# Two transformer blocks on one core: x normalised and modulated beside the memory units, the memory keys later, two more steps in each attention head, and the last norm's row loaded later

## The reference

```
# first block
mod = silu(c) @ w_ada + b_ada                 # 2048 x 12288: six rows of 2048
shift_m, scale_m, gate_m, shift_f, scale_f, gate_f = split(mod, 6)
h = rmsnorm(x, g_norm_mix) * (1 + scale_m) + shift_m
dq, dk, dv, q_lat, kv_lat, k_pe = split(h @ w_in)
o_diff = 8 heads: (softmax(q1 k1) - lam * softmax(q2 k2)) @ v, then a norm
q = rmsnorm(q_lat) @ w_q_b;  kv = rmsnorm(kv_lat) @ w_kv_b
o_mla = 8 heads: softmax(q k) @ v
x = x + gate_m * (concat(o_diff, o_mla) @ w_out)
h = rmsnorm(x, g_norm_ffn) * (1 + scale_f) + shift_f
x = x + gate_f * (square(relu(h @ w_ff1)) @ w_ff2)      # 2048 -> 8192 -> 2048
x = rmsnorm(x, g_final)
# second block
proj = rms_norm(x) @ w_in_2       # q, k, v, z of three branches and three gates of 2048
ya = 12 heads, sliding window of 128, with sinks
yb = 12 heads, causal with forgetting
mk, mv = split(rms_norm(mem) @ w_mem_kv)                # 256 memory tokens
yc = 4 heads: softmax(norm(qc) norm(mk)) @ mv
y = sum over branches of sigmoid(gate) * ((y_branch * silu(z)) @ w_branch)
out = x + y @ w_out_2
```

## Time and profile before

| | before |
|---|---|
| median of three runs | 2192.8 us (2191.8 to 2196.15) |
| profiled execution, its span | 2190.42 us, 2188.6 us |
| mean granted clock of TensorE | 0.961 |
| busy: PE, DVE, ACT, POOL | 2000.1 (91%), 1313.3 (60%), 945.3 (43%), 157.9 us (7%) |
| moved by DMA | 448.82 MB, 205 GB/s in the mean |
| memory tiles 15 and 16 done at | 93.1 and 96.6 us |
| x times rx on ScalarE (L698), first two pieces of eight | 1.33 us, from 95.35 |
| waits of PE on heads, 262 to 411.6 us, beside the one in the rows | 0.15, 2.52 and 1.64 us for pt; 1.48 for probs |
| waits of PE on heads of branches a and b | 2.63 for pt; 1.42 and 0.44 for probs; 2.59 for the reciprocal; 2.71 and 1.57 for z |
| PE busy in 620 to 660 us (first tiles of w_ff1) | 18.89 and 18.41 of 20 us each |

### The profile page before, as it was taken

How to read it: one execution, slowest core, us unless ns; L and a number is a source line. 1 busy time by engine, 2 the same in 40 slices (tenths; PEclk the granted TensorE clock), 3 DMA queues, 4 the chain that set the end, 5 groups by cost and what they waited for, 6 DMA issues and landing times. The chain is left out here.

```text
span 2188.6 us, 24524 instructions
## 1 busy us (share of the span) xinstructions
PE 2000.1 (91%) x9240; PEld 1642.4 (75%) x9240; DVE 1313.3 (60%) x2057; ACT 945.3 (43%) x1440; POOL 157.9 (7%) x118
## 2 busy tenths in 40 slices
PE   6598897867789999999999999979999999999999
PEld 3276775546667888888888878878988877787877
DVE  3777876776796555555555555566555545545544
ACT  2453445343444344434434455445444444444433
POOL 0100000001000110110010021110100001101000
PEclk9798999878999999999999999989999999999999
DMA  9798775657797555555555555434534456656644
GB/s 356 284 327 307 244 250 199 235 189 278 290 340 255 192 192 184 192 193 186 188 193 187 187 193 179 149 100 126 164 108 149 126 169 198 192 182 187 194 170 170
DMA packets 128967, 448.82 MB, mean 205 GB/s; under 512 B 14288, under 2 KB 14544, under 8 KB 128336
## 3 DMA queue, kind: packets, MB, share of 16 engines
q1 hardware_dynamic: 124928, 433.74, 59.8%
q0 software_dynamic: 1568, 7.34, 0.9%
q10 hardware_dynamic: 2352, 6.17, 0.7%
HBM read 443.00 MB, written 4.19 MB: 204 GB/s over the span
## 5 line engine op out<-in xcount | busy, mean ns | idle before, releaser
L283 DVE TENSOR_TENSOR wlo<-raw,whi 128x1024 fp32r<-128x1024 f32 (+4 forms) x652 | 784.9, 1208 | 750.3 <-ACT whi L282 695.5
L282 ACT ACTIVATE whi<-raw 128x1024 fp32r<-128x1024 f32 (+4 forms) x652 | 658.3, 1012 | 836.6 <-PE g L397 707.0
L392 PE MATMUL g<-whi,lhsA_hi 128*128 128x512 f32 (+4 forms) x1840 | 715.8, 391 | 35.6 <-DVE lhsA_lo L788 28.0
L393 PE MATMUL g<-whi,lhsA_lo 128*128 128x512 f32 (+4 forms) x1840 | 698.0, 381 | 0.0
L397 PE MATMUL g<-wlo,lhsA_hi 128*128 128x512 f32 (+4 forms) x1840 | 470.0, 378 | 0.2 <-DVE wlo L283 0.2
L392 PEld LDWEIGHTS g<-whi,lhsA_hi 128*128 128x128 f32 x1840 | 357.3, 194 | 99.0 <-ACT tmp L780 21.8
L393 PEld LDWEIGHTS g<-whi,lhsA_lo 128*128 128x128 f32 x1840 | 357.6, 194 | 53.8 <-issue 1.4
L397 PEld LDWEIGHTS g<-wlo,lhsA_hi 128*128 128x128 f32 x1840 | 344.4, 193 | 56.2 <-DVE wlo L283 0.4
L537 DVE SCALAR_TENSOR_TENSOR raw<-raw,srow 128x1024 f32<-128x1024 f32 x181 | 217.5, 1224 | 17.8 <-DMA raw<-in_w_ada 17.5
L392 PE MATMUL g<-whi,lhsF_hi 128*128 128x512 f32 x512 | 200.6, 392 | 0.0
L393 PE MATMUL g<-whi,lhsF_lo 128*128 128x512 f32 x512 | 199.4, 389 | 0.0
(11 more groups left out here) (250 smaller groups left out, 1471.8 us busy)
## 6 DMA issues: line engine op xcount, KB each, us to landing
raw<-in_w_ff SPq DMA_DIRECT2D x256, 512.0 KB, 3.5
raw<-in_w_ada SPq DMA_DIRECT2D x181, 512.0 KB, 4.8
raw<-in_w_in SPq DMA_DIRECT2D x176, 512.0 KB, 4.2
raw<-in_w_out SPq DMA_DIRECT2D x64, 512.0 KB, 5.0
raw<-in_w_in SPq DMA_DIRECT2D x80, 384.0 KB, 3.1
raw<-in_w_branch_a SPq DMA_DIRECT2D x12, 512.0 KB, 3.5
raw<-in_w_branch_b SPq DMA_DIRECT2D x12, 512.0 KB, 4.3
raw_wide<-in_w_ada SPq DMA_DIRECT2D x11, 512.0 KB, 7.6
```

The lines of the kernel that those rows point to most:

```text
L282: t_hi = AC.put(lambda e: e.activation(hi, x, ACT.Copy), landed, free, us=0.2 + n * 0.00167)
L283: t_lo = DV.put(lambda e: e.tensor_tensor(lo, x, hi.bitcast(F32), ALU.subtract), landed, t_hi, free, us=0.15 + n * 0.00208)
L392: PE.put(lambda e, o=o, x=xh, w=h, f=first: e.matmul(o, x, w, start=f, stop=False), w, mark=False, us=us)
L393: PE.put(lambda e, o=o, x=xl, w=h: e.matmul(o, x, w, start=False, stop=False), mark=False, us=us)
```

## The change

Four edits, no new arithmetic.

1. row_norms(xs) and the eight `modulated` generators are appended before the first memory unit is run, so that they run beside the memory units; a `modulated` step now also waits until its piece of xs is scaled. angles() and lam() stand behind the second memory unit. The memory keys (mem_keys) are appended behind both units, with four `yield`s more, so that they come in w_in.
2. In diff_head and in softmax_pv a `yield` is put ahead of taking bank T and another ahead of taking bank O; the same two in causal_head. Each head's chain is two steps longer.
3. g_final is no longer loaded beside x, but behind the eight adds of w_out, when spread(1) has been appended.

```
-    for j in range(8):
-        bg.append(mem_turned(j))
-    bg.append(row_norms(ms, t_m, ssm, rm, "rm"))
...
-    par, tok = run(u_mem[0], width=3, adas_per_pair=2)
-    drain()
-    r = take(rows)
-    ks = evac2(par, tok, 512, r.ap, t_of["rm"], r.free, scale=(rm[:, 0:1], rm[:, 1:2]))
-    bg.append(mem_keys(r, ks))
-    bg.append(row_norms(xs, t_x, ssx, rx, "rx"))
-    angles()
-    lam()
-    par, tok = run(u_mem[1], adas_per_pair=2)
-    t_of["mv"] = evac2(par, tok, 512, mv, t_of["rm"], scale=(rm[:, 0:1], rm[:, 1:2]))
-    narrow()
-    while ("xs", 3) not in t_of:
-        pump()
...
     def modulated(j, src, src_tok, sec, ready=None):
...
-        while any(c not in ada_done for c in cs):
+        while any(c not in ada_done for c in cs) or (sec == 0 and ("xs", j // 2) not in t_of):
             yield
...
     for j in range(8):
+        bg.append(mem_turned(j))
+    bg.append(row_norms(ms, t_m, ssm, rm, "rm"))
+    bg.append(row_norms(xs, t_x, ssx, rx, "rx"))
+    for j in range(8):
         bg.append(modulated(j, [xs[:, t, (2 * j + i) * P:(2 * j + i + 1) * P] for i in range(2) for t in range(2)],
                             lambda j=j: t_of["xs", j // 2], 0))
...
+    def mem_keys(r, tok):
+        yield from heads_norm(r, 4, 128, tok)
+        for _ in range(4):
+            yield
...
+    par, tok = run(u_mem[0], width=3, adas_per_pair=2)
+    while "rm" not in t_of:
+        pump(1, 3)
+    r = take(rows)
+    ks = evac2(par, tok, 512, r.ap, t_of["rm"], r.free, scale=(rm[:, 0:1], rm[:, 1:2]))
+    par, tok = run(u_mem[1], width=3, adas_per_pair=2)
+    t_of["mv"] = evac2(par, tok, 512, mv, t_of["rm"], scale=(rm[:, 0:1], rm[:, 1:2]))
+    narrow()
+    angles()
+    lam()
+    while ("xs", 3) not in t_of:
+        pump(1, 3)
+    bg.append(mem_keys(r, ks))
...
@@ reload
         x_tok.extend([t_xr] for _ in range(4))
-        t_of["gfin"] = load(PO, gfin, a["g_final"].rearrange("(a d) -> a d", a=1).to_broadcast([P, D]), w)
...
     bg.append(spread(1, [DV.tok()]))
+    t_of["gfin"] = load(PO, gfin, a["g_final"].rearrange("(a d) -> a d", a=1).to_broadcast([P, D]), fence)
```

More of the change, by code:

```diff
@@ L708, in mem_turned, with modulated @@
                    [t_vec])
+    def modulated(j, src, src_tok, sec, ready=None):
+        cs = [4 * sec + (sec // 2) * 4 + j // 2, 4 * sec + (sec // 2) * 4 + 4 + j // 2]
+        wanted[j] = cs
+        while any(c not in ada_done for c in cs) or (sec == 0 and ("xs", j // 2) not in t_of):
+            yield
+        b = yield from grab(SOB)
+        tok = turn_rows(b, src, src_tok())
+        yield
+        tm = yield from grab(tmps)
+        for i in range(2):
+            kk = 2 * j + i
+            gcol, scol = mods[:, 16 * (sec + 1) + kk:][:, 0:1], mods[:, 16 * sec + kk:][:, 0:1]
+            tt = AC.put(lambda e, i=i, g=gcol, s=scol: e.activation(
+                tm.ap[:, 256 * i:256 * i + 256], b.ap[:, 256 * i:256 * i + 256], ACT.Identity, bias=s, scale=g),
+                tok, tm.free, [ada_done[c] for c in cs])
+        b.release([tt])
+        hi = lhsA.hi[:, 2 * j:2 * j + 2, :].rearrange("p a b -> p (a b)")
+        lo = lhsA.lo[:, 2 * j:2 * j + 2, :].rearrange("p a b -> p (a b)")
+        th = AC.put(lambda e: e.activation(hi, tm.ap[:, :], ACT.Copy), tt, lhsA.free)
+        yield
+        tl = DV.put(lambda e: e.tensor_tensor(lo, tm.ap[:, :], hi.bitcast(F32), ALU.subtract), th, lhsA.free)
+        tm.release([tl])
+        lhsA.ready[j] = tl
     for j in range(8):
@@ L712, in build @@
     bg.append(row_norms(ms, t_m, ssm, rm, "rm"))
+    bg.append(row_norms(xs, t_x, ssx, rx, "rx"))
+    for j in range(8):
+        bg.append(modulated(j, [xs[:, t, (2 * j + i) * P:(2 * j + i + 1) * P] for i in range(2) for t in range(2)],
+                            lambda j=j: t_of["xs", j // 2], 0))
     def heads_norm(r, segs, width, tok, off=0):
@@ L752, in build @@
     par, tok = run(u_mem[0], width=3, adas_per_pair=2)
-    drain()
+    while "rm" not in t_of:
+        pump(1, 3)
     r = take(rows)
     ks = evac2(par, tok, 512, r.ap, t_of["rm"], r.free, scale=(rm[:, 0:1], rm[:, 1:2]))
-    bg.append(mem_keys(r, ks))
-    bg.append(row_norms(xs, t_x, ssx, rx, "rx"))
+    par, tok = run(u_mem[1], width=3, adas_per_pair=2)
+    t_of["mv"] = evac2(par, tok, 512, mv, t_of["rm"], scale=(rm[:, 0:1], rm[:, 1:2]))
+    narrow()
     angles()
     lam()
-    par, tok = run(u_mem[1], adas_per_pair=2)
-    t_of["mv"] = evac2(par, tok, 512, mv, t_of["rm"], scale=(rm[:, 0:1], rm[:, 1:2]))
-    narrow()
     while ("xs", 3) not in t_of:
-        pump()
-    def modulated(j, src, src_tok, sec, ready=None):
-        cs = [4 * sec + (sec // 2) * 4 + j // 2, 4 * sec + (sec // 2) * 4 + 4 + j // 2]
-        wanted[j] = cs
-        while any(c not in ada_done for c in cs):
[L772 to L790, removed]
-    for j in range(8):
-        bg.append(modulated(j, [xs[:, t, (2 * j + i) * P:(2 * j + i + 1) * P] for i in range(2) for t in range(2)],
-                            lambda j=j: t_of["xs", j // 2], 0))
+        pump(1, 3)
+    bg.append(mem_keys(r, ks))
     fence = [PE.tok(), AC.tok(), DV.tok(), PO.tok()]
```

## The result

The changed kernel takes 2214.4 us (median of four runs, 2209.8 to 2215.66), the kernel before 2192.3 (four runs). The ratio is 1.0094 with an interval of 1.0078 to 1.0110: 21 us slower, where 2184 was forecast, and outside the stated range.

The account below looks back on a forecast made before the run. TensorE, busy 2000 of 2188.6 us, was taken to bound the kernel. -3.6 - 8 + 10 - 2 - 4 - 1.5 = -9.1 us from 2190.4 gives 2181.3; the median lies 2.4 higher, so 2184, range 2170 to 2202.

Parts of the forecast that it names:

- Part 1: Start and w_in, with x beside the memory units: -7.9 us by tile 4, +3.9 and 0.4 later, in sum -3.6.
- the second wait: TensorE's wait before tile 31 of w_in: nine adas (VectorE passes over w_ada tiles) instead of four, +3.9 us.
- The bound of +6.4 for transfers: Upper bound for the added wait before tile 31 of w_in: five transfers at 410 GB/s, 1.28 us each.
- Part 2, heads ahead of wlo 80: Heads from 262 to 411.6 us: the added steps remove waits for pt and probs, -8 us, between 0 and -11.
- no change: Rival: new waits give back Part 1, heads' waits move from pt to bank pO; within 4 us of 2193; chance 0.15.
- Part 2, the tail: From wlo 80 to x's load: 54 adas instead of 39 make VectorE lengthen it, +10 us, between +2.5 and +18.
- the tail decides: Rival, slower: VectorE's idle time stays, so the stretch from wlo 80 to x's load grows 18 us; about 2201; chance 0.20.
- half of the old idle time stays: Between wlo 80 and x's load: half of VectorE's 15.4 us idle remains, taking its 107.1 us to 114.6.
- The rival's sentence that waits cost twice there: Rival that heads' waits go and the tail stays: clock 0.85 shows waits cost twice; about -20, 2172; chance 0.27.
- Fewer adas in w_ff1: First tiles of w_ff1, 620 to 660 us: 12 adas already done early shorten TensorE's waits, -2 us.
- Branches: Branches a and b: steps reach 7.1 us of waits for pt, probs and the reciprocal; -4 us, between +2 and -10.
- Part 3: Load of x near 517 us: without g_final's 1 MB beside it x lands sooner, -1.5 us, from 0 to -2.6.

Follow-up runs that it names:

- kernel 2: Kernel before with both added steps (ahead of taking banks T and O) in diff_head and the mla heads alone; 2216.2 us, ratio 1.0118.
- 13: As 11, but the planner lets an ada end only 2 us behind TensorE, not 3, between wlo 80 and 92; 2183.7 us, ratio 0.9967.
- 5: As kernel 2, but a head leaves the steps out while the planner pumps without a weight tile; 2214.1 us, ratio 1.0112.
- 12: As kernel 2, but the planner lets an ada end 2 us behind TensorE, not 3, between wlo 80 and 92; 2210.0 us, ratio 1.0087.
- 15: Kernel before with both steps in the mla heads alone; 2203.7 us, ratio 1.0065.
- 6: Kernel before with only the step ahead of taking bank T, in diff_head and the mla heads; 2199.2 us, ratio 1.0038.
- 7: Kernel before with only the step ahead of taking bank O, in diff_head and the mla heads; 2196.2 us, ratio 1.0026.
- 11: Changed kernel without the first block's head steps; planner lets an ada end 6 us behind TensorE, not 3, in w_in tiles 3 to 33; 2183.3 us, 0.9972.
- kernel 14: Kernel before with both steps in diff_head alone; 2192.1 us, ratio 1.0011.

## Why the prediction was wrong

**Part 1, predicted -3.6, measured +2 (ratio 1.0009, with an interval that reaches just under 1).** The mechanism was right at each step of the start. The first tile of w_in was forecast at 102.7 and started at 104.12, and tile 4, forecast at 114.6, started at 115.87. The step that failed is the second wait: nine adas were costed at VectorE's pace, 1.19 us each, with its idle time there for free. VectorE in the changed kernel, the first and the last of the nine:

```profile
195.85 1.23 DVE L537 SCALAR_TENSOR_TENSOR raw<-raw,srow 128x1024 f32<-128x1024 f32 x1 [0.98 <-DMA raw<-in_w_ada]
...
206.57 1.22 DVE L537 SCALAR_TENSOR_TENSOR raw<-raw,srow 128x1024 f32<-128x1024 f32 x1
```

Nine take 11.9 us from start to end; before needed 5.3 us for its four. The last eight start 1.28 us apart, which is what 512 KB take at the 410 GB/s of the earlier trace rows, where VectorE can start one every 1.15 us once they have landed (542.43, 543.58 and 544.72 in the same trace). So the transfers set the pace. Tile 4 gained 6.6 us and not 7.9, and the wait behind tile 30 grew by 7.9 us, where the sum had 3.9 and 0.4 for the keys' transposes. The bound of +6.4 for transfers was in the text; the middle of the range should have been there.

**Part 2, heads ahead of wlo 80, predicted -8, measured +0.6** (150.2 in place of 149.6). The waits for pt went, as said. What failed is "what is taken away isn't refilled": I looked for VectorE to refill it, and it was mostly the banks pO and pT, 9.6 us of waits in this stretch. The stretch has 33 matmuls fewer besides, which went to the tail, so +0.6 flatters it. The rival "no change" named it, pt to bank pO, and was given 0.15.

**Part 2, the tail, predicted +10, measured +35.** That is where the forecast failed. The rival "the tail decides" was the right one, with its condition met (more than 19 us over the 104.6), and it too was sized too small, at +18. The 15 adas were as computed, 17.6 us, but 4.8 us of other work of VectorE moved in, which the sum did not have. So the step that failed is the rest of the term: "half of the old idle time stays" gave 7.7 us, and VectorE's idle time nearly doubled, to 28.4 us, while TensorE waited 16 us in this stretch for the banks pO and pT, which the sum did not have. And no term of the sum held the clock. The matmuls behind the waits of the changed kernel, first the waits and then one pair of score matmuls, and below it such a pair in the kernel before:

```profile
414.64 0.66 PE L450 MATMUL pT<-cst,probs 128*128 128x128 f32 x4 [1.71 <-ACT pt L933]
417.76 2.08 PE L939 MATMUL pO<-region,pt 128*128 128x128 f32 x8 [2.46 <-ACT pO L947]
...
421.53 2.08 PE L1013 MATMUL pO<-region,pt 128*128 128x128 f32 x8 [0.84 <-ACT pO L947]
...
424.42 2.05 PE L1013 MATMUL pO<-region,pt 128*128 128x128 f32 x8 [0.81 <-ACT region L1025]
...
428.39 1.22 PE L975 MATMUL pS<-region 128*128 128x256 f32 x2
```

```profile
412.60 0.70 PE L971 MATMUL pS<-region 128*128 128x256 f32 x2
```

Two waits of 1.71 and 2.46 us (and two of 0.8 behind them) were followed by 25 us in which matmuls ran at the lower level: a pair of score matmuls took 1.22 us and not 0.70, and eight such pairs stood there. In before they stood ahead of the waits, at full clock, the last of them ending at 413.9. A and B together, in the kernel before and then in kernel 2:

```profile
254.23:516.89 262.66, 205.64 (x920) 155.59 (x918) 199.21 (x424) 113.60 (x289) 0.00 (x0) 0.89 0.66 225
```

```profile
255.53:554.08 298.55, 223.32 (x923) 169.12 (x922) 217.07 (x456) 115.44 (x289) 0.00 (x1) 0.82 0.63 221
```

Kernel 2 takes 35.9 us longer there, of them 18.2 us idle of TensorE (57.0 to 75.2) and 17.7 us busy (205.6 to 223.3), for 923 matmuls in place of 920. So half of the loss is waits, and nearly all of the other half is the same work run at a lower clock. The rival's sentence that waits cost twice there fits these numbers, and its use was wrong: it was counted as a gain to come. The rule cited from the Trainium skill ("TensorE: Matmul & The Clock Gate", "HAM oscillation — how this bites in real kernels"), that idle gaps make TensorE slow afterwards, agrees with the 0.54 of these 30 us; I had weighed it for the 10 us wait of Part 1 alone.

**Fewer adas in w_ff1, predicted -2,** was right in kind and small in size: 4 us came back in the changed kernel between x's load and branch a, though no run shows that it was the adas alone, and in 13 the reverse took all of the 11 us.

**Branches, predicted -4, measured -4.6** (0.9979). Right in size, and the waits that were named did go, but part of the size is luck: the waits of P*V for z (2.71 and 1.57), forecast to stay, went too, and 7.4 us of new ones came (for lb L1427 and for small L1401), which no term had. The heads there have one bank pT and one bank pO too, and four probs buffers of half the size in place of two; their waits still did not move to the banks, but for one of 1.5 us for pT. Why the same steps win there and lose in the first block was not tried.

**Part 3, predicted -1.5,** measured -2.4 (0.9989) with an interval that reaches just past 1, and no mechanism in the trace: x lands in 11.1 us without g_final and in 11.2 with it. That x landed in 10.2 us in the changed kernel, as forecast, was luck: in kernel 2, which loads g_final behind it, it took 10.1. By these traces the term should have been 0, its lower end. The sentence of the Trainium skill cited there ("DMA: Bandwidth & Descriptors", "Issuing engines are not separate DMA queues") has transfers interleave; the runs show no delay of x by it here, and why wasn't looked for.

**What stays open.** It stays open why the two steps in the mla heads bring the clock down and those in diff_head don't, and why both kinds together cost 10 us more than the sum of each alone. The kernels with the fall (2, 5, 12, 15) all have the pause of the mla heads' tails behind tile 80; two others with pauses of these tails (6 and 7) kept 0.87 from 400 to 440. An order that differed in this pause alone wasn't tried.

## What to carry to other kernels

A step more in a chain took the waits for pt away here, and in the first block waits for banks came in their place: before adding a step, count the banks of each kind and ask who holds them one step later. And where waits of TensorE come to stand close together, add the clock to the bill: price what follows at its slow duration from a row, not at its mean.

Work that one stage does for a later one (here w_ada tiles) is only lent: 11 tiles fewer in kernel 13 shortened the stage by 11 us and cost 11 us in the next. The fastest of these kernels are the change without the first block's steps, with the 6 us limit (11, 0.9972) and with the 2 us limit besides (13, 0.9967): 6 to 7 us faster than before, and not to be told from each other.

## What the runs showed of the hardware

In the changed kernel four pauses of 1.71, 2.46, 0.84 and 0.81 us were followed by 19 us at half clock, from 424.42 to 443.6, the first 12 of them without a pause (22.9 us busy in the 30 us at 0.54). In kernel 14 pauses of 2.81, 0.77, 0.77 and 2.79 us were followed by one slow tile, of 4.6 us, and then by full clock. The kernel before has five pauses of 0.77 to 2.81 us between 415 and 431.3 us, 8.6 us in sum, and one slow tile behind them. So slow stretches differ by a factor of four behind pauses of much the same sum or less, and nothing in the rows says why.
